# Second pass of a fused RWKV-7, attention and mixture-of-experts layer: transposed inverse in banks of its own, products of head groups and levels interleaved

## What is computed

```python
def step(state, inp):
    r_t, w_t, k_t, v_t, a_t, b_t = inp
    sa = jnp.einsum('bhvk,bhk->bhv', state, a_t)
    state = (state * w_t[:, :, None, :] + sa[..., None] * b_t[:, :, None, :]
             + v_t[..., None] * k_t[:, :, None, :])
    y = jnp.einsum('bhvk,bhk->bhv', state, r_t)
    return state, y
```

## Time and profile before

| | us |
|---|---|
| median of 3 runs | 2917.29 (2915.37 to 2919.76) |
| profiled execution | 2919.52 |
| its span, first to last instruction | 2917.7 |
| PE busy | 2523.9 (87%) |
| DVE busy | 1076.8 (37%) |
| ACT busy | 741.6 (25%) |
| POOL busy | 404.5 (14%) |
| mean granted clock of PE | 0.924 |

### The profile page before, as it was taken

One profiled execution on the slowest core, in us unless ns is written; L12 is line 12 of the kernel. 1 busy time (PEld: TensorE's weight loads), 2 busy tenths in 40 slices (PEclk: granted clock), 3 DMA queues, 4 the chain that ended last, 5 costly groups with the idle time before them and its releaser, 6 DMA issues. The chain is left out here.

```text
span 2917.7 us, 68706 instructions
## 1 busy us (share of the span) xinstructions
PE 2523.9 (87%) x28364; PEld 1606.3 (55%) x28365; DVE 1076.8 (37%) x2618; ACT 741.6 (25%) x1797; POOL 404.5 (14%) x455
## 2 busy tenths in 40 slices
PE   6899999999997789999999995499999699988920
PEld 1788888889886467777776763223332133322300
DVE  0154444544545245555555554111111011111118
ACT  1234344343443112222232320112222122212200
POOL 0121212212221021212121210000000000000013
PEclk7899999999998899999999996699999899999965
DMA  8012112111123823232323220848419977588567
GB/s 309 24 44 84 48 44 88 45 76 56 45 81 118 336 78 116 91 118 89 111 89 110 89 75 29 352 167 333 162 46 364 391 304 298 218 330 350 223 280 281
DMA packets 59264, 473.40 MB, mean 162 GB/s; under 512 B 8284, under 2 KB 8800, under 8 KB 38400
## 3 DMA queue, kind: packets, MB, share of 16 engines
q1 hardware_dynamic: 39672, 405.07, 35.8%
q0 software_dynamic: 9936, 36.18, 3.5%
q10 hardware_dynamic: 9440, 28.99, 2.6%
HBM read 374.92 MB, written 95.29 MB: 161 GB/s over the span
## 5 line engine op out<-in xcount | busy, mean ns | idle before, releaser
L1716 PE MATMUL ps<-arena 128*32 128x512 f32 x4608 | 531.5, 620 | 71.5 <-DMA arena<-wex 71.5
L443 PE MATMUL ps<-arena 128*128 128x128 f32 (+2 forms) x3584 | 420.1, 276 | 2.1 <-ACT arena L592 2.1
L443 PEld LDWEIGHTS ps<-arena 128*128 128x128 f32 (+2 forms) x3584 | 407.3, 187 | 16.8 <-ACT arena L592 12.8
L1716 PEld LDWEIGHTS ps<-arena 128*32 128x32 f32 x4608 | 153.0, 114 | 443.6 <-issue 387.8
L1100 PE MATMUL ps<-arena 64*64 64x64 f32 x8704 | 295.6, 221 | 27.7 <-ACT arena L1303 9.5
L1100 PEld LDWEIGHTS ps<-arena 64*64 64x64 f32 x8704 | 275.5, 136 | 56.7 <-issue 55.4
L1730 PE MATMUL ps<-arena 128*32 128x512 f32 x2304 | 265.4, 602 | 17.8 <-DMA arena<-wex 17.5
L1245 PE MATMUL ps<-arena 128*128 128x512 f32 x512 | 238.8, 610 | 0.7 <-ACT arena L1322 0.7
L1931 DVE TENSOR_TENSOR arena<-arena,ps 128x256 f32<-128x256 f32 x72 | 29.9, 416 | 507.4 <-ACT arena L1775 507.4
L1775 ACT ACT_TABLE_LOAD x36 | 46.2, 1283 | 657.2 <-PE ps L1716 657.2
L454 PE MATMUL ps<-arena 128*128 128x256 f32 (+1 forms) x512 | 174.3, 489 | 0.0
(11 more groups left out here) (312 smaller groups left out, 3065.3 us busy)
## 6 DMA issues: line engine op xcount, KB each, us to landing
arena<-wex SPq DMA_DIRECT2D x108, 2048.0 KB, 9.7
mid<-arena SPq DMA_DIRECT2D x16, 2568.0 KB, 8.5
arena<-mid SPq DMA_DIRECT2D x16, 2568.0 KB, 10.3
arena<-ada SPq DMA_DIRECT2D x12, 2048.0 KB, 10.8
y<-arena ACTq DMA_DIRECT2D x36, 512.0 KB, 8.0
arena<-x SPq DMA_DIRECT2D x32, 512.0 KB, 5.4
arena<-w_in SPq DMA_DIRECT2D x8, 1232.0 KB, 19.9
y<-arena SPq DMA_DIRECT2D x16, 512.0 KB, 11.5
```

Of the source, the lines that this page charges most:

```text
L443: mm = pe.matmul(bank[name][0:m, at:at + P], V["w_in"][:, kk, w0:w0 + m], V["hT"][:, kk, :], start=(kk == 0), stop=(kk == KD - 1))
L1716: mm = pe.matmul(bank[("HA", "HB")[g]][rows[j], :], xT[:, kk, rows[j]], slot[j][:, at:at + 2 * FH], start=(kk == 0), stop=(kk == KD - 1))
```

## The change

The transposed inverse gets banks of its own: XT of group 0 goes to YE, of group 1 to YO, each as one more use (xT1 to xT5) ahead of y; X stays in X0 and X1 and has no use at the last level. ACT copies X and XT by an instruction each (128x256). The PE steps Z2 to Z5 are gone from PE; their products are made in the step X of the level below, so that X(l) is: x of group 0, xT of group 0, x of group 1, z of the next level of group 0, xT of group 1, z of the next level of group 1. Z1 stays a step. ORDER is not changed; DVE and POOL keep their steps Z1 to Z5 where they stood. The number of products is the same.

```diff
@@ -933,9 +933,9 @@
 _LV = range(1, len(LEVELS))
 USES2 = {"Z0": ("M", *(f"z{l}" for l in _LV), "G", "U0", "U1"),
          "Z1": ("M", *(f"z{l}" for l in _LV), "I", "U0", "U1"),
-         "X0": ("M", "t0", *(f"x{l}" for l in _LV), "WT"),
-         "X1": ("M", "t0", *(f"x{l}" for l in _LV), "WT", "D0", "D1"),
-         "YE": ("y",), "YO": ("y",),
+         "X0": ("M", "t0", *(f"x{l}" for l in _LV[:-1]), "WT"),
+         "X1": ("M", "t0", *(f"x{l}" for l in _LV[:-1]), "WT", "D0", "D1"),
+         "YE": (*(f"xT{l}" for l in _LV), "y"), "YO": (*(f"xT{l}" for l in _LV), "y"),
          "O0": ("yT", "o", "hT", "rl"), "O1": ("yT", "o", "hT")}
 BANK2 = {b: i for i, b in enumerate(("O0", "O1", "Z0", "Z1", "X0", "X1", "YE", "YO"))}
 
@@ -984,6 +984,7 @@
     hs = lambda h: slice(HD * h, HD * h + HD)
     by_head = lambda ap: ap.rearrange("p (c e n) -> p c e n", c=CC, e=2)
     M_BANKS = (("Z0", "Z1"), ("X0", "X1"))
+    XT_BANKS = ("YE", "YO")
     MODS = len(ADA_PIECES) - MOD1
 
     def once(step):
@@ -1091,16 +1092,14 @@
                                         B.full(mm, name)
                 return go
 
-            def blocks(name, lhs, rhs, heads, at=0, first=True, last=True):
-
-                if first:
-                    pe.sem_inc(S["pe_passed"], 1)
+            def blocks(name, lhs, rhs, heads):
+
+                pe.sem_inc(S["pe_passed"], 1)
                 for i, h in enumerate(heads):
                     for rows in chunk:
-                        mm = pe.matmul(bank[name][rows, at + CHUNK * i:at + CHUNK * i + CHUNK], lhs(rows, h), rhs(rows, h),
+                        mm = pe.matmul(bank[name][rows, CHUNK * i:CHUNK * i + CHUNK], lhs(rows, h), rhs(rows, h),
                                        start=True, stop=True)
-                if last:
-                    B.full(mm, name)
+                B.full(mm, name)
 
             def x2(n, b):
                 for g in range(2):
@@ -1108,27 +1107,41 @@
                     B.wait_free(pe, f"X{g}", "t0", n)
                     blocks(f"X{g}", XT, lambda rows, h: k("ident64")[rows, :], range(4 * g, 4 * g + 4))
 
-            def Zl(l):
+            def z_part(n, l, g):
+                S.wait(pe, "et" if l > 1 else "et1", 4 * n + l - 1 if l > 1 else 2 * n + g + 1)
+                B.wait_read(pe, f"X{g}", f"x{l - 1}" if l > 1 else "t0", n)
+                B.wait_free(pe, f"Z{g}", f"z{l}", n)
+                blocks(f"Z{g}", lambda rows, h: ET[l][rows, h, :], X, range(4 * g, 4 * g + 4))
+
+            def x_part(n, l, g):
+                if l == 1:
+                    B.wait_read(pe, f"X{g}", "t0", n)
+                else:
+                    B.wait_read(pe, XT_BANKS[g], f"xT{l - 1}", n)
+                B.wait_read(pe, f"Z{g}", f"z{l}", n)
+                if l < last:
+                    B.wait_free(pe, f"X{g}", f"x{l}", n)
+                    blocks(f"X{g}", XT, lambda rows, h: Z[rows, h, :], range(4 * g, 4 * g + 4))
+
+            def xT_part(n, l, g):
+                B.wait_free(pe, XT_BANKS[g], f"xT{l}", n)
+                blocks(XT_BANKS[g], lambda rows, h: Z[rows, h, :], XT, range(4 * g, 4 * g + 4))
+
+            def Z1(n, b):
+                for g in range(2):
+                    z_part(n, 1, g)
+
+            def Xl(l):
+
                 def go(n, b):
-                    if l > 1:
-                        S.wait(pe, "et", 4 * n + l - 1)
-                    for g in range(2):
-                        if l == 1:
-                            S.wait(pe, "et1", 2 * n + g + 1)
-                        B.wait_read(pe, f"X{g}", f"x{l - 1}" if l > 1 else "t0", n)
-                        B.wait_free(pe, f"Z{g}", f"z{l}", n)
-                        blocks(f"Z{g}", lambda rows, h: ET[l][rows, h, :], X, range(4 * g, 4 * g + 4))
-                return go
-
-            def Xl(l):
-                def go(n, b):
-                    for g in range(2):
-                        heads = range(4 * g, 4 * g + 4)
-                        B.wait_read(pe, f"Z{g}", f"z{l}", n)
-                        B.wait_free(pe, f"X{g}", f"x{l}", n)
-                        if l < last:
-                            blocks(f"X{g}", XT, lambda rows, h: Z[rows, h, :], heads, last=False)
-                        blocks(f"X{g}", lambda rows, h: Z[rows, h, :], XT, heads, at=256, first=(l == last))
+                    x_part(n, l, 0)
+                    xT_part(n, l, 0)
+                    x_part(n, l, 1)
+                    if l < last:
+                        z_part(n, l + 1, 0)
+                    xT_part(n, l, 1)
+                    if l < last:
+                        z_part(n, l + 1, 1)
                 return go
 
             def Wg(n, b):
@@ -1139,7 +1152,7 @@
             def Wt(n, b):
                 pk = W["pk"][b]
                 for g in range(2):
-                    B.wait_read(pe, f"X{g}", f"x{last}", n)
+                    B.wait_read(pe, XT_BANKS[g], f"xT{last}", n)
                 for q in range(2):
                     B.wait_free(pe, f"X{q}", "WT", n)
                 pe.sem_inc(S["pe_passed"], 1)
@@ -1281,7 +1294,7 @@
                         mm = pe.matmul(bank["O1"][:, :], k("every32"), rows, start=True, stop=True)
                     mm.then_inc(S["mod_T"], 1)
 
-            run(pe, {**mods(mod), "Ma": M(0), "Mb": M(1), "x2": x2, **{f"Z{l}": Zl(l) for l in _LV}, **{f"X{l}": Xl(l) for l in _LV},
+            run(pe, {**mods(mod), "Ma": M(0), "Mb": M(1), "x2": x2, "Z1": Z1, **{f"X{l}": Xl(l) for l in _LV},
                      "Wg": Wg, "Wt": Wt, "Wi": Wi, "Yv": Yv,
                      **{f"S{q}{'ab'[part]}": scan(q, part) for q in range(2) for part in range(2)}, "yT": yT,
                      **{f"o{8 * n0 + kk}": o(n0, kk) for n0 in range(2) for kk in range(KD)}, "h2T": h2T,
@@ -1295,12 +1308,11 @@
                     B.free(act.activation(XX[:, g, 0, :], bank[f"X{g}"][:, 0:256], ACT.Copy), f"X{g}")
 
             def Xl(l):
-                o = 1 if l == last else 0
-
                 def go(n, b):
-                    for g in range(2):
-                        B.wait_full(act, f"X{g}", f"x{l}", n)
-                        B.free(act.activation(XX[:, g, o:, :], split(bank[f"X{g}"][:, 256 * o:], 2 - o), ACT.Copy), f"X{g}")
+                    for o, g in ((0, 0), (1, 0), (0, 1), (1, 1)) if l < last else ((1, 0), (1, 1)):
+                        name, use = (f"X{g}", f"x{l}") if o == 0 else (XT_BANKS[g], f"xT{l}")
+                        B.wait_full(act, name, use, n)
+                        B.free(act.activation(XX[:, g, o, :], bank[name][:, 0:256], ACT.Copy), name)
                 return go
 
             def Wg(n, b):
```

## The result

The changed kernel takes 2937.57 us (median of 6 runs, 2934.46 to 2950.24) against 2918.13 us before (2915.37 to 2924.79): ratio 1.0071, 95% interval 1.005 to 1.0091. It is slower by some 20 us, where 2912.5 us had been forecast in a range of 2903 to 2922. The profiled execution took 2940.62 us, with a span of 2938.8 us, its clock 0.918 for 0.924.

A forecast was written before the change was run, and what follows sets the result against it. PE's own work was taken to bound the second pass. Gains of 2.8 us (14 tiles) and 2.4 us (tile 1), less 0.4 us for waits and increments, made 4.8 us: 2912.5 us by the median, range 2903 to 2922.

The forecast's parts named there:

- Structure: Second pass, per tile: regular gaps of 1.71 us go, new waits of 1.50 us come, about 0.2 us gained.
- the route wait: Between route and X5: PE waits for DVE's Z5, queued behind the router step; 0.92 us lost per tile.
- New waits: PE waits 0.36 us ahead of X2, 0.21 us in X4 and 0.92 us behind route; together 1.50 us per tile.
- Tile 1 and tile 0: Tiles off the pattern: tile 1 gains 2.4 us, tile 0 gains 0 with bounds -1 and +1 us.
- YE and YO, Yv and ACT's longer copies: Banks and copies: 1.4 us more of ACT per tile, cost 0; without Wg as cover 0.73 us per tile.
- Idle that waits for nothing visible: PE's issue idle in the second pass, pieces up to 1.4 us: no change taken, bounds -4 and +5 us.
- rival C: Without the gaps' supply time, PE's issue idle returns: 11 us slower, 2928 us; sign turns at 0.37 us per tile; chance 0.12.
- a run of 96 loads keeps the pace of one of 32: PE's weight loads in one tile's inversion: longer runs show no slowing, held against returning issue idle.
- Item 2: About 30 more PE waits and increments per tile: 0.03 us per tile taken, bounds 0 and 0.3 us.

The follow-up runs named there:

- e3_route: The changed kernel with DVE's router step moved behind its Z5; 2918.32 us, ratio 1.0002.
- e5_lean: e3_route without PE's already covered waits and the increments at XT of levels 2 to 5, 24 semaphore instructions fewer per tile; 2905.88 us, 0.9948.
- e11_wait: The kernel before with only PE's Z5 moved ahead of route, DVE's order kept; 2950.06 us, 1.01.
- e9_lean_only: The changed kernel with e5_lean's waits and increments dropped on PE, DVE's router step left ahead of Z5; 2933.59 us, 1.0049.
- e4_shift: The changed kernel with 128 semaphore increments on PE once, at the start of the second pass; 2958.57 us, 1.014.
- e12_spread2: e5_lean with output products spread between inversion levels, h2 directly behind h2T and route four product steps later; 2925.76 us, 1.0016.
- e6_traffic: e3_route with an unused load of 2 MB more per tile from tile 3 on; 2919.43 us, 0.9997.
- e2_incs: The kernel before with 22 more semaphore increments per tile on PE, ahead of the X products; 2943.11 us, 1.0084.
- e1_banks: The changed kernel's banks and four ACT copies per level, but PE in the order of before; 2932.54 us, 1.0043.
- e10_before_lean: The kernel before with 18 covered waits per tile dropped on PE, only 4 instructions per tile gone; 2918.8 us, 0.9999.

## Why the prediction was wrong

- **Structure: right.** Without the route wait the forecast was 1.71 - 0.36 - 0.21 = 1.14 us per tile net; e3_route shows 1.43 from x2 to Wg, and 1.67 with M. New waits 0.36 + 0.21 + 0.92 forecast, 0.24, 0.15 and 0.84 measured. Tile 1 and tile 0 together 2.4 forecast, 2.42 measured. YE and YO, Yv and ACT's longer copies cost nothing that a wait shows.
- **The step that failed: "Idle that waits for nothing visible. I take no change", bounds -4 and +5 us.** It grew by 1.30 us per tile (1.60 to 2.90), 17 us in 13 tiles, and e3_route isolates it: 1.67 us per tile gained, 1.32 back as stalls. That is near rival C, which had 0.12, in kind and size: C needed 0.37 us per tile to turn the sign and took 1.03. But C put it down to the gaps alone, and e5_lean shows the whole to need the added semaphore instructions too (1.71 against 1.60 before). C's own sum also has a slip: its 0.4 us are a cost, not a gain, and the 2.4 us of tile 1 are left out. The evidence I held against it, that a run of 96 loads keeps the pace of one of 32, spoke of the wrong scale, since the period of the stalls is some 122 loads. The list of waits had the sign: the pieces of up to 1.4 us were at changing places, since the tile's 1844 instructions are no multiple of 256. The single timeline I read was one without such a stall up to X5.
- **The wait of 0.92 us was priced as idle time only.** What it did to the clock was not in the sum: some 7 us by the medians of e3_route and the changed kernel (19.2 less 11.8), 13.7 us in the changed kernel's profiled execution. e11_wait shows it in the kernel before: 29 us slower, where the waits put in, less the gap that went, come to 14.6 us.
- **Item 2, waits and increments, 0.03 us taken, bounds 0 and 0.3 us per tile.** The 30 further waits and increments are 22 further instructions in the trace (74 for 52), some carrying two waits. In the dense new order they weigh: 24 instructions fewer give 12.4 us by the medians (e5_lean), 0.9 us per tile; the upper bound was three times too low. The reason given (borders inside a run show no cost) holds within the run that was read, but the cost comes as stalls elsewhere. It is largely the same time as in the step above (the irregular part falls by 1.21 of the 1.30 us that it had grown), not a second loss beside it.
- **The sum.** In 13 tiles of the profiled executions, 16.9 us of stalls, 10.9 of the wait behind route, 13.7 of the clock, less 21.7 of regular gain gives +19.8 us; measured are +22.1 there and +19.4 in the medians of the whole kernel. The 2.3 us left are not split further. The clock's part differs from one execution to another (2 stretches in the profiled execution of e9_lean_only, its fastest).
- The Trainium skill (Runtime: NRT & Kernel Launch, Instruction fetch mechanics) says that fetch goes in blocks of 256 instructions, and that the crossing is mostly hidden. The first half agrees with the index of the late loads here (34 of 38). The second agrees in part: 61 of the 95 such places show no late load, and at the others up to 2.4 us are lost. That the fetch itself is the cause is argued from the period, from e4_shift and from e12_spread2; no record of it is in the trace. Why it is late is open; e6_traffic shows that 41 GB/s of further transfers don't change it.

The version to take is e5_lean: the interleaving, with the router step out of the way and the covered waits gone, 2905.88 us, 0.5% below the kernel before.

## What to carry to other kernels

Before closing gaps between short products, look in the list of waits for "issue" pieces and count at how many instructions they recur. Here closed gaps and 22 more semaphore instructions per tile together brought stalls that took back most of the gain; over the whole tile closed gaps with few such instructions added 0.11 us of them (e5_lean), and many such instructions in open gaps none (e2_incs). Price a wait on PE for another engine by what the clock does behind it as well as by its length, and look which step of the reader's queue stands between. When gaps are closed, drop the semaphore instructions that an earlier wait covers, and count them in the trace, since one instruction can carry two waits. What that brings while the gaps are there stays open.

## What was not expected of the hardware

- PE's stream of mostly 64x64 float32 products stalls at one place in 256 instructions, for 0.2 to 2.4 us, at about a third of these places in the changed kernel (34 of 95 in 13 tiles) and a quarter before (22 of 93). The places move with the instruction count (e4_shift) and ignore 41 GB/s of added DMA (e6_traffic).
- A semaphore increment on PE that nothing covers took 0.15 us (128 in 19.6 us, e4_shift; two in 0.30 us, e2_incs).
- At a wait of 0.84 to 0.93 us between route and X5 the granted clock fell to 1.2 GHz for 3.41 or 6.83 us, in 8 of 14 tiles of the changed kernel and, with a further 0.5 us of waits ahead of route, in 11 of 14 of e11_wait; 64 loads then took 2.79 to 3.52 us instead of 1.97. It doesn't fall each time, and what decides that is open. It also fell without such a wait, behind late loads close to route: three times in e1_banks (1.13 to 1.73 us late), twice in e3_route, once each in e5_lean and e10_before_lean.
